# Where the eight attention up matmuls of a pair stand: two blocks of four, or one at each of eight places in the doubling levels

## The chip, the core and the metric

The kernel runs on one core of one Trainium2 chip. The metric is the device time of one execution in microseconds (us), and three runs of the kernel before the change took 1629.02, 1631.33 and 1635.49 us (median 1631.33). The engines are TensorE (PE in the profile; its weight loads are PEld), VectorE (DVE), ScalarE (ACT), GpSimd (POOL) and SyncE (SP), which here only issues DMAs. They work in parallel and wait for each other through semaphores; each of them takes its own instructions in program order.

## The reference, cut to what matters

One trunk layer over 384 tokens (128 context tokens and 256 latent ones, three tiles of 128): a norm and a combined input projection, two token mixers beside each other (a bidirectional RWKV-7 scan and grouped-query attention), a gated merge, and then top-4-of-32 experts. The part around the change is the mixer's end:

```
y_r, s_f, s_b = rwkv7_bidir(r, k, v, (wd_f, wd_b), (ad_f, ad_b), gd, (s0_f, s0_b), lp)
...
y_a = block_attention(rope_2d(qh), k_all, v_all)
merged = (jax.nn.sigmoid(gate_r) * (y_r @ lp["w_up_r"])
          + jax.nn.sigmoid(gate_a) * (y_a @ lp["w_up_a"]))
return merged @ lp["w_out"], kh, vh, s_f, s_b
```

The scan of one step is `S = S * w_t - (S kk_t) (kk_t a_t)^T + v_t k_t^T`, once forward and once backward over each sequence. The changed matmuls are `y_a @ w_up_a`: (384 x 512) by (512 x 1024), all fp32.

## The kernel before, in words

The program runs in stages: modulation, the input projection with the attention woven in (up to about 280 us), the RWKV scans (about 280 to 494 us), the merge and output projection (to about 563 us), second norm, router and placement (to about 620 us), and the expert blocks, which stream some 400 MB of weights.

The scans are written in chunk form, and run in three pairs (`pairs`). A pair p is one tile for the forward direction (d = 0) and one for the backward direction (d = 1). `bk(d, i)` is PSUM bank 4d + i, so each direction has four of the eight banks. A pair goes through these steps, on PE with the helpers `mm` and `quads`:

- the small low-rank matmuls (banks 4d and 4d + 1) for decay and in-context rate, then the cumulative sums (`cum`, `colm`), between them and after them elementwise work on DVE (L1728 to L1752) and exponentials on ACT (L1346 to L1351);
- 32 transposes (L722), copied out by ACT, and 64 Gram matmuls, which DVE masks into `AM` (L1760);
- one `quads` group for each direction into bank 4d + 3. A `quads` group is 16 fp32 matmuls of 64 x 64, which use quarters of the array;
- the doubling levels, l = 1 to 5 (`LEVELS` is 6), which invert a triangular matrix. In each level PE runs a group P for d = 0 and for d = 1 (bank 4d, operands `AM` and `XM`), and then a group D for d = 0 and for d = 1 (bank 4d + 2, operands `PM` and `XT`). DVE makes `PM[d]` from P's bank by a mask (L1777), makes the new `XT[d]` by subtracting D's bank (L1781), and turns it into `XM[d]` (L1784), which the next level's P waits for. Before the first level DVE makes the first `XT` (L1766, L1767) and the first `XM` (L1769);
- the state matmuls of two chunks, whose results DVE and ACT take up.

Into this sequence the attention's up matmuls were put, since they depend on none of it. For one tile they are eight: two column halves n of 512, each an accumulation of four (k = 0 to 3) over a stationary 128 x 128 block of `yaT` (in `first`) with a moving 128 x 512 of `w_up_a` (in `ring`). `up_a(j, n, bank)` did one half, by `up_half`, four matmuls in a row; ACT's `raised` copied the bank to `upa_out[j]` in `zbuf`. In pair 0 both halves stood between the last `quads` group and the first level. In pairs 1 and 2 half 0 stood behind the low-rank matmuls and half 1 before the first level. The order on each engine is that of the code; there is no planner. In the records of the trace one fp32 matmul is two MATMUL records (and two LDWEIGHTS), so a `quads` group is x32, and half an up projection x8.

What hangs on the end of the scans: everything behind them on PE, ACT, DVE and SP waits for `yrd` to reach 12, the last of the chunk results. The issue of the second half of `w_out`, `weights(("out", 1))` at L510, waits for `upad` to reach 6, all six up halves.

Of the kernel before, what the change touches and what calls it, by code (L numbers as in the profile page):

```python
# [29 lines left out]
P = 128  # L30
D = 1024
KC = D // P
NT = 3
# [21 lines left out]
CH = 512  # L55
# [18 lines left out]
LEVELS = 6  # L74
# [11 lines left out]
SLOT = KC * CH  # L86
# [71 lines left out]
def build(nc, a, o):  # L158
    ctx = ExitStack()
    with ctx:  # L160
# [216 lines left out]
        def landed(eng, key):  # L377
            i = turn[key]
            eng.wait_ge(s_wld[i % 3], 16 * (i // 3 + 1))
# [333 lines left out]
        def _(pe):  # L713
# [174 lines left out]
            def up_half(key, src, j, n, bank):  # L888
                w = at(ring, (turn[key, 0] + 1) % 3 * SLOT, 4, D)
                for k in range(4):  # L890
                    last = mm(bank, src[:, k, j * P:(j + 1) * P], w[:, k, n * CH:(n + 1) * CH], k == 0, k == 3)
                return last

            def up_a(j, n, bank):
                if j == n == 0:
                    landed(pe, ("upa", 0))
                    pe.wait_ge(S["yTc"], NT)
                up_half("upa", yaT, j, n, bank).then_inc(S["upad"], 1)

# [3 lines left out]
            for p, pair in enumerate(pairs):  # L903
# [8 lines left out]
                if p == 0:  # L912
                    turn_attended()
                else:
                    up_a(p, 0, bk(1, 2))
                for d, j in pair:
                    u = 2 * p + d
                    pe.wait_ge(S["lw"], u + 1)
                    if p == 0:
                        pe.wait_ge(S["yTc"], (1, NT)[d])  # L920
                    elif d == 1:
                        pe.wait_ge(S["yTc"], NT + 2 * p + 1)
                    mm(bk(d, 3), cum[:, 2 * d + 1, :], LW[d]).then_inc(S["lcum"], 1)
                    mm(bk(d, 2), cum[:, 2 * d, :], LW[d]).then_inc(S["lcum"], 1)
                    for c in range(4):
                        last = mm(bk(d, 0)[:, 4 * c:4 * c + 4], LW[d][:, c * P:(c + 1) * P], colm[:, 4 * d:4 * d + 4])
                    last.then_inc(S["lcum"], 1)
# [27 lines left out]
                if p == 0:  # L955
                    up_a(0, 0, bk(0, 1))
                    up_a(0, 1, bk(1, 1))
                else:
                    up_a(p, 1, bk(0, 1))
                for l in range(1, LEVELS):  # L960
                    for d, j in pair:
                        pe.wait_ge(s_x[d], NX * p + 2 * l)
                        if l > 1:
                            pe.wait_ge(s_pc[d], NP * p + l - 1)
                        quads(bank_block(bk(d, 0)), blocks(AM[d], 0), blocks(XM[d])).then_inc(s_p[d], 1)
                    for d, j in pair:
                        pe.wait_ge(s_pc[d], NP * p + l)
                        quads(bank_block(bk(d, 2)), blocks(PM[d]), blocks(XT[d])).then_inc(s_d[d], 1)
                pe.wait_ge(S["yTc"], NT + 2 * p + 2)
                for d, j in pair:  # L970
# [260 lines left out]
        def _(sc):  # L1231
# [101 lines left out]
            for p, pair in enumerate(pairs):  # L1333
# [4 lines left out]
                if p == 0:  # L1338
                    for j in range(NT):
                        turned(j, (B[2], B[7], B[6])[j], tile_of(yaT, j))  # L1340
                else:
                    raised(p, 0, bk(1, 2))
                for d, j in pair:
# [14 lines left out]
                for d, j in pair:  # L1358
                    sc.wait_ge(s_u[d], 3 * p + 1)
                    cp(flat(GM[d]), bk(d, 3)).then_inc(s_uc[d], 1)  # L1360
                if p == 0:
                    raised(0, 0, bk(0, 1))
                    raised(0, 1, bk(1, 1))
                else:
                    raised(p, 1, bk(0, 1))
                for d, j in pair:
# [766 lines left out]
```

## Time and profile before

| | us |
|---|---|
| median of three runs | 1631.33 |
| the profiled execution | 1628.82 |
| its span in the trace | 1626.9 |
| PE busy, share of the span | 1469.4, 90% |
| DVE busy | 524.0, 32% |
| ACT busy | 262.1, 16% |
| scans, from the first pair's levels to their end | about 305 to 494 |

A row of the timeline says when a run of like instructions began, how long it took, its engine, line, operation, tiles and count, and in brackets how long the engine had been idle before it and which instruction ended that idle time. A row of the chain gives start, duration and what the end of the program was waiting for in that stretch. Times in the rows are microseconds from the start of the span. L715 is the line inside `mm`, L719 that inside `mm_part`, L722 that inside `tr`; L1232 is ACT's copy helper.

### The profile page before, as it was taken

What the parts mean: (1) busy time and instruction counts of PE and PEld (TensorE: products, weight loads), DVE (VectorE), ACT (ScalarE), POOL (GpSimd) and SP (SyncE); (2) the same over time, 40 slices, a digit from 0 to 9 for tenths busy, and PEclk for the clock granted to TensorE, in tenths of its full rate; (3) what the DMA queues carried; (4) which work ended last, traced back from release to release, by engine and by line L of the source; (5) the groups of instructions that cost most, each with busy time, mean ns of one, the idle gap of its engine ahead of it and who ended that gap; (6) DMA issues with size and microseconds to landing.
All of it is one profiled execution on the core that took longest, in us unless ns stands there. A gap on an engine that the chain in (4) does not pass through costs nothing.

```text
span 1626.9 us, 26117 instructions
## 1 busy us (share of the span) xinstructions
PE 1469.4 (90%) x10008; PEld 706.3 (43%) x10009; DVE 524.0 (32%) x976; ACT 262.1 (16%) x514; POOL 98.9 (6%) x191
## 2 busy tenths in 40 slices
PE   4899998988987967999989999999998998998994
PEld 1777666777684442333323333333332332332331
DVE  3464544777877542101101101101011010110126
ACT  0332333221301200101101101111011010110110
POOL 1000000000001000000000000000000000000011
PEclk8799999999997967999999999999999999999996
DMA  9556835000016486999999999999999999999995
GB/s 364 200 189 239 324 133 187 2 9 3 2 55 220 171 329 272 421 421 421 421 421 421 421 422 420 422 421 421 421 420 423 420 421 420 419 421 419 419 411 190
DMA packets 97928, 510.78 MB, mean 314 GB/s; under 512 B 14752, under 2 KB 17072, under 8 KB 45160
## 3 DMA queue, kind: packets, MB, share of 16 engines
q1 hardware_dynamic: 82392, 479.03, 72.5%
q10 hardware_dynamic: 10624, 18.23, 3.0%
q0 software_dynamic: 4848, 12.59, 2.1%
q8 instruction: 50, 0.82, 0.2%
q14 instruction: 14, 0.11, 0.0%
HBM read 491.03 MB, written 22.71 MB: 316 GB/s over the span
## 4 chain that ended last, share of the span: by engine, by line
PE 60%; DMA 16%; SPq 10%; DVE 10%; issue 3%; ACT 1%; POOL 0%; DVEq 0%; ACTq 0%; POOLq 0%
PE bank L715 47%; PE bank L719 10%; SPq L594 9%; DMA ring<-w_moe_in 5%; DMA work<-w_moe_in 3%; DMA spare<-w_moe_in 3%; PE bank L722 3%; DMA zbuf<-w_ada 1%; DVE work L2051 1%; DMA work<-rows_d,dest 1%; DVE work L1781 1%; DMA work<-mods_d 1%; DVE work L1760 1%; DVE work L2052 1%; DVE work L1784 1%
## 5 line engine op out<-in xcount | busy, mean ns | idle before, releaser
L715 PE MATMUL bank<-work 64*64 64x64 f32 (+3 forms) x5134 | 528.9, 353 | 38.4 <-DMA work<-w_moe_in 11.2
L715 PEld LDWEIGHTS bank<-work 64*64 64x64 f32 (+2 forms) x5134 | 243.9, 136 | 286.5 <-issue 231.8
L715 PE MATMUL bank<-ring,work 128*64 128x512 f32 (+1 forms) x1376 | 352.8, 607 | 17.1 <-DMA ring<-w_moe_in 11.0
L2045 DVE TENSOR_SCALAR work<-bank 128x512 f32<-128x512 f32 x39 | 27.0, 692 | 753.1 <-PE bank L715 753.1
L715 PEld LDWEIGHTS bank<-ring,work 128*64 128x64 f32 (+1 forms) x1376 | 115.1, 145 | 224.9 <-issue 192.3
L1232 ACT ACTIVATE work<-bank 128x512 f32<-128x512 f32 (+2 forms) x223 | 110.8, 512 | 568.9 <-PE bank L715 323.3
L719 PE MATMUL bank<-parts 128*128 128x512 f32 (+1 forms) x720 | 168.1, 388 | 2.9 <-DVE parts L448 2.9
L715 PE MATMUL bank<-zbuf,work 64*64 64x64 f32 (+2 forms) x966 | 138.4, 388 | 12.5 <-DMA zbuf<-w_moe_in 4.5
L719 PEld LDWEIGHTS bank<-parts 128*128 128x128 f32 x720 | 129.3, 191 | 33.9 <-issue 5.2
L1462 ACT ACTIVATE work<-work 128x512 f32<-128x512 f32 x39 | 24.6, 630 | 469.8 <-DVE work L2045 469.8
L715 PEld LDWEIGHTS bank<-zbuf,work 64*64 64x64 f32 (+2 forms) x966 | 63.8, 139 | 77.0 <-issue 59.7
L722 PE MATMUL bank<-ident,work 128*128 128x128 f32 (+1 forms) x340 | 68.5, 319 | 22.1 <-DVE work L2052 11.2
L448 DVE TENSOR_TENSOR parts<-ring,parts 128x1024 fp32r<-128x1024 f32 (+1 forms) x40 | 45.7, 1145 | 76.7 <-ACT parts L443 76.7
L722 PEld LDWEIGHTS bank<-ident,work 128*128 128x128 f32 (+1 forms) x340 | 47.9, 179 | 49.6 <-DVE work L2052 32.5
L715 PE MATMUL bank<-spare,work 128*64 128x512 f32 (+1 forms) x256 | 61.3, 557 | 3.8 <-ACT work L1232 2.1
L680 POOL TENSOR_TENSOR half<-half 128x1 f32<-128x1 f32 x38 | 7.0, 183 | 847.0 <-PE bank L722 834.1
L715 PE MATMUL bank<-first,work 128*64 128x512 f32 x208 | 52.6, 607 | 2.0 <-DMA first<-w_moe_in 2.0
L443 ACT ACTIVATE parts<-ring 128x1024 fp32r<-128x1024 f32 (+1 forms) x40 | 39.6, 994 | 77.4 <-PE bank L719 73.6
L2051 DVE TENSOR_SCALAR work<-bank 128x256 f32<-128x256 f32 x78 | 32.9, 421 | 57.2 <-PE bank L715 57.2
L667 POOL DMA_INDIRECT zbuf<-h_d,slots x39 | 40.9, 1050 | 19.8 <-issue 19.8
L722 PEld LDWEIGHTS bank<-ident,zbuf 128*128 128x128 f32 x204 | 23.6, 150 | 41.8 <-issue 37.7
L715 PE MATMUL bank<-rowc 96*64 96x512 bf16 x234 | 39.9, 392 | 1.8 <-issue 1.8
(261 smaller groups left out, 859.8 us busy)
## 6 DMA issues: line engine op xcount, KB each, us to landing
work<-w_moe_in SPq DMA_DIRECT2D x108, 1024.0 KB, 22.8
ring<-w_moe_in SPq DMA_DIRECT2D x84, 1024.0 KB, 25.5
work<-w_moe_out SPq DMA_DIRECT2D x64, 1024.0 KB
ring<-w_moe_out SPq DMA_DIRECT2D x44, 1024.0 KB, 21.3
ring<-w_ada SPq DMA_DIRECT2D x11, 2048.0 KB, 7.7
zbuf<-w_moe_in SPq DMA_DIRECT2D x22, 1024.0 KB
first<-w_moe_in SPq DMA_DIRECT2D x21, 1024.0 KB
spare<-w_moe_in SPq DMA_DIRECT2D x21, 1024.0 KB
```

The source lines that it names most:

```text
L443: nc.scalar.activation(zpart(t, 0, n), z_quarter(t), ACT.Copy).then_inc(S["hi"], 1)
L448: eng.tensor_tensor(zpart(t, 1, n), z_quarter(t), zpart(t, 0, n), ALU.subtract)\
L594: sp.dma_start(place_of(turn_e, c), src).then_inc(s_place[(WC * turn_e + c) % NPLACE], 16)
L667: gp.indirect_dma_start(xg, None, h2_d.rearrange("t (h n) -> (t h) n", h=2), bass.IndirectOffsetOnAxis(ap=slots[:, 0:1], axis=0), bounds_c ...
L715: return pe.matmul(out, l, r, start=start, stop=stop)
L719: return pe.matmul(out, l, r, start=start, stop=stop, skip_group_check=True)
L722: return pe.transpose(out, src, ident[0:n, 0:n])
L1232: cp = lambda out, src, scale=1.0: sc.activation(out, src, ACT.Copy, scale=scale)
L1462: sc.activation(th, gl, ACT.Tanh, scale=ALPHA / 2).then_inc(S["thd"], 1)
L1760: tt(dst, bk(d, 2 * par + i).rearrange("p (c n) -> p c n", c=2), gramm[:, d:d + 1, :].broadcast_to([P, 2, 4 * HC]), M).then_inc(S["am"], 1)
L2045: ts(gl, B[0], LIMIT, None, ALU.min).then_inc(S["thd"], 1)
L2051: LL(ts(uu[:, seg], B[1][:, seg], LIMIT, -LIMIT, ALU.min, ALU.max))
```

## The change

The up matmuls of a pair are issued one by one: in each of the levels 1 to 4, one (half 0, k = l - 1, bank 1) between the P groups and the D groups, and one (half 1, bank 5) behind the D groups. `up_a` now takes k, and issues one matmul through `mm_part`, which is `mm` without the check that accumulation groups don't interleave; the instruction is the same. Level 5 has none. Half 0 of pairs 1 and 2 goes from behind the low-rank matmuls to the levels. ACT copies both halves behind the copies of `GM`, in every pair. The wait on `yTc` that protected bank 6 is gone with the half that used it. The number of matmuls and of copies is the same.

```
-            def up_a(j, n, bank):
-                if j == n == 0:
-                    landed(pe, ("upa", 0))
-                    pe.wait_ge(S["yTc"], NT)
-                up_half("upa", yaT, j, n, bank).then_inc(S["upad"], 1)
+            def up_a(j, n, k):
+                w = at(ring, (turn["upa", 0] + 1) % 3 * SLOT, 4, D)
+                ins = mm_part(bk(n, 1), yaT[:, k, j * P:(j + 1) * P], w[:, k, n * CH:(n + 1) * CH], k == 0, k == 3)
+                if k == 3:
+                    ins.then_inc(S["upad"], 1)
...
                 if p == 0:
                     turn_attended()
-                else:
-                    up_a(p, 0, bk(1, 2))
                 for d, j in pair:
                     u = 2 * p + d
                     pe.wait_ge(S["lw"], u + 1)
                     if p == 0:
                         pe.wait_ge(S["yTc"], (1, NT)[d])
-                    elif d == 1:
-                        pe.wait_ge(S["yTc"], NT + 2 * p + 1)
...
                 if p == 0:
-                    up_a(0, 0, bk(0, 1))
-                    up_a(0, 1, bk(1, 1))
-                else:
-                    up_a(p, 1, bk(0, 1))
+                    landed(pe, ("upa", 0))
                 for l in range(1, LEVELS):
                     for d, j in pair:
                         pe.wait_ge(s_x[d], NX * p + 2 * l)
                         if l > 1:
                             pe.wait_ge(s_pc[d], NP * p + l - 1)
                         quads(bank_block(bk(d, 0)), blocks(AM[d], 0), blocks(XM[d])).then_inc(s_p[d], 1)
+                    if l < LEVELS - 1:
+                        up_a(p, 0, l - 1)
                     for d, j in pair:
                         pe.wait_ge(s_pc[d], NP * p + l)
                         quads(bank_block(bk(d, 2)), blocks(PM[d]), blocks(XT[d])).then_inc(s_d[d], 1)
+                    if l < LEVELS - 1:
+                        up_a(p, 1, l - 1)
...
@@ (ScalarE)
-                else:
-                    raised(p, 0, bk(1, 2))
...
-                if p == 0:
-                    raised(0, 0, bk(0, 1))
-                    raised(0, 1, bk(1, 1))
-                else:
-                    raised(p, 1, bk(0, 1))
+                for n in range(2):
+                    raised(p, n, bk(n, 1))
```

On PE, at the start of pair 1's levels, this stood before. Banks 0 and 4 take the P groups of the two directions, banks 2 and 6 the D groups, `ring,first` marks the up matmuls, and a row x16 is one `quads` group:

```order
L715 MATMUL bank3<-zbuf,work 64x64 x16
L715 MATMUL bank7<-zbuf,work 64x64 x16
L715 MATMUL bank1<-ring,first 128x512 x4
L715 MATMUL bank0<-work 64x64 x16
L715 MATMUL bank4<-work 64x64 x16
L715 MATMUL bank2<-work 64x64 x16
L715 MATMUL bank6<-work 64x64 x16
L715 MATMUL bank0<-work 64x64 x16
L715 MATMUL bank4<-work 64x64 x16
```

At the same place of PE's program now:

```order
L715 MATMUL bank7<-zbuf,work 64x64 x16
L715 MATMUL bank0<-work 64x64 x16
L715 MATMUL bank4<-work 64x64 x16
L719 MATMUL bank1<-ring,first 128x512
L715 MATMUL bank2<-work 64x64 x16
L715 MATMUL bank6<-work 64x64 x16
L719 MATMUL bank5<-ring,first 128x512
L715 MATMUL bank0<-work 64x64 x16
L715 MATMUL bank4<-work 64x64 x16
L719 MATMUL bank1<-ring,first 128x512
```

The block of four ahead of the first P group is gone, and one up matmul stands between each two P groups and the D groups behind them, another behind the D groups.

At the start of pair 1, behind the low-rank matmuls (`spare` into banks 0, 4, 1, 5), PE had half 0 in bank 6 ahead of the cumulative sums:

```order
L715 MATMUL bank1<-spare 128x512
L715 MATMUL bank5<-spare 128x512
L715 MATMUL bank6<-ring,first 128x512 x4
L715 MATMUL bank3<-work,spare 128x512
L715 MATMUL bank2<-work,spare 128x512
L715 MATMUL bank0<-colm,work 128x4 x4
```

And now:

```order
L722 MATMUL bank4<-ident,work 64x128 x4
L715 MATMUL bank0<-spare 128x512
L715 MATMUL bank4<-spare 128x512
L715 MATMUL bank1<-spare 128x512
L715 MATMUL bank5<-spare 128x512
L715 MATMUL bank3<-work,spare 128x512
```

The cumulative sums follow the low-rank matmuls directly.

## Rows read from the trace of the kernel before

**Rows 1.** The page, part 4: the chain that ended last, by engine.
```profile
PE 60%; DMA 16%; SPq 10%; DVE 10%; issue 3%; ACT 1%; POOL 0%; DVEq 0%; ACTq 0%; POOLq 0%
```

**Rows 2.** The chain in order of time, one level of pair 1: start, duration, what.
```profile
384.01 2.11 PE bank L715 x64
...
386.14 0.70 DVE work L1781
...
386.90 0.60 issue
387.50 0.66 DVE work L1781
...
388.18 0.72 DVE work L1784
...
388.95 2.11 PE bank L715 x64
```

**Rows 3.** Timeline of PE, pair 1, up half 1 and the first levels.
```profile
373.36 1.15 PE L715 MATMUL bank<-zbuf,work 64*64 64x64 f32 x32 [1.24 <-DVE work L1760]
374.43 3.70 PE L715 MATMUL bank<-ring,first 128*128 128x512 f32 x8
378.06 4.02 PE L715 MATMUL bank<-work 64*64 64x64 f32 x128
...
384.01 3.09 PE L715 MATMUL bank<-work 64*64 64x64 f32 x96 [0.17 <-DVE work L1784]
387.63 1.15 PE L715 MATMUL bank<-work 64*64 64x64 f32 x32 [0.53 <-DVE work L1784]
```

**Rows 4.** Timeline of DVE, pair 1: first XM, first and last XT of d = 0.
```profile
374.66 0.71 DVE L1769 STREAM_TRANSPOSE work<-work 128x512 f32<-128x512 f32 x1
...
376.71 0.71 DVE L1769 STREAM_TRANSPOSE work<-work 128x512 f32<-128x512 f32 x1
...
381.20 0.69 DVE L1781 TENSOR_TENSOR work<-work,bank 128x512 f32<-128x512 f32 x1 [0.32 <-PE bank L715]
...
400.95 0.69 DVE L1781 TENSOR_TENSOR work<-work,bank 128x512 f32<-128x512 f32 x1 [0.24 <-PE bank L715]
```

**Rows 5.** Timeline of PE, pair 0, both up halves.
```profile
298.49 7.13 PE L715 MATMUL bank<-ring,first 128*128 128x512 f32 x16
305.56 0.62 PE L715 MATMUL bank<-work 64*64 64x64 f32 x14
```

**Rows 6.** Timeline of DVE, pair 0: the second first XM, the first XT subtraction.
```profile
300.76 0.71 DVE L1769 STREAM_TRANSPOSE work<-work 128x512 f32<-128x512 f32 x1
...
308.69 0.69 DVE L1781 TENSOR_TENSOR work<-work,bank 128x512 f32<-128x512 f32 x1 [0.32 <-PE bank L715]
```

**Rows 7.** Timeline of DVE, pair 2, the same two.
```profile
446.07 0.71 DVE L1769 STREAM_TRANSPOSE work<-work 128x512 f32<-128x512 f32 x1
...
450.57 0.69 DVE L1781 TENSOR_TENSOR work<-work,bank 128x512 f32<-128x512 f32 x1 [0.32 <-PE bank L715]
```

**Rows 8.** Timeline of PE, pair 2, inside its second level.
```profile
456.39 1.84 PE L715 MATMUL bank<-work 64*64 64x64 f32 x55 [0.56 <-issue]
```

**Rows 9.** Timeline of PE, pair 1: the 32 transposes ahead of the Gram matmuls.
```profile
363.44 3.82 PE L722 MATMUL bank<-ident,work 128*128 128x128 f32 x32
```

**Rows 10.** Timeline of DVE, pair 1: the last product that is transposed.
```profile
365.86 0.68 DVE L1745 TENSOR_TENSOR work<-zbuf,work 128x512 f32<-128x512 f32 x1
```

**Rows 11.** Windows: busy us of PE, PEld, DVE, ACT, POOL (records), granted clock, DMA.
```profile
347.90:354.40 6.50, 5.23 (x16) 2.43 (x16) 1.61 (x3) 1.62 (x3) 0.00 (x0) 0.50 0.20 43
416.00:422.00 6.00, 5.22 (x126) 5.09 (x124) 3.37 (x8) 0.98 (x4) 0.00 (x0) 1.00 0.02 4
487.90:508.10 20.20, 13.91 (x63) 8.63 (x62) 15.18 (x28) 0.60 (x1) 2.46 (x2) 0.58 0.50 158
```

**Rows 12.** The chain, behind the output projection.
```profile
564.74 16.23 DMA work<-mods_d
```

**Rows 13.** The page, part 6: loads of 2 MB into a ring slot, us to landing.
```profile
ring<-w_ada SPq DMA_DIRECT2D x11, 2048.0 KB, 7.7
```

## The prediction

> **What bounds the kernel now.** I read the page's chain first: PE carries 60% of it, DVE 10%, DMA and its issue 26% [rows 1]. Most of that is the expert stage, which the change does not touch. It matters only that every stage behind the scans starts from their end (`yrd`), so that a microsecond gained or lost in the scans should reach the end of the program.
>
> Then the chain inside one doubling level of pair 1, between one start of P(d=1) and the next [rows 2]. Two `quads` groups on PE, P(d=1) and D(d=0), take 384.01 to 386.14; DVE then subtracts for d=0 (386.14), turns it, subtracts for d=1 (387.50) and turns that (388.18), and P(d=1) of the next level starts at 388.95. A level is 4.94 us, and in it PE and DVE take turns. The reader is to see that DVE's subtraction for d=0 is released by D(d=0), and that D(d=0) stands directly behind P(d=1) on PE: the three groups P(d=1), D(d=0), D(d=1) run without a break (3.09 us, x96), while PE's idle time lies behind the D groups, 0.53 us, and between the two P groups, 0.17 us [rows 3]. So of the two new places in a level, the one behind the D groups has 0.7 us of idle time to fill, and the one between P and D has none: it stands on the chain.
>
> **What one up matmul costs.** Eight in a row took 298.49 to 305.56, 7.07 us [rows 5]; four in a row took 374.43 to 378.06, 3.63 us [rows 3]. The difference gives 0.86 us for one inside a block, and leaves 0.19 us that each block pays once. One more piece: a lone group lasts 1.15 us from its first start to its last result, while groups in a row follow each other by (3.09 - 1.15)/2 = 0.97 us; but the up block started 1.07 us behind the group ahead of it (373.36 to 374.43) [rows 3], so the entry costs 0.10 us more. A single up matmul among `quads` groups is then S = 0.86 + 0.19 + 0.10 = 1.15 us of PE. The trace has no lone one. The bounds: 0.86 us, if nothing is paid at the change; and 0.86 + 0.29 + 2 x 0.18 = 1.51 us, if on both sides the 0.18 us by which a group's last result trails its spacing (1.15 - 0.97) is waited out on top. I take 1.15, since both blocks, of four and of eight, stood between `quads` groups too and agree on it.
>
> The Trainium skill, TensorEngine Tiling (Array Packing), section Tiling Modes, says that a change of the tiling mode, not of the tile alone, drains the engine. This speaks against the change, which makes 24 excursions out of the levels' 64 x 64 mode where there were three; the rows show 0.29 us for one excursion, which fits that rule. Without a drain the price would be the low bound.
>
> **A level with its two up matmuls.** I count from the start of P(d=1). By DVE: group 0.97, up 1.15, D(d=0) until its last result 1.15, release 0.01, which puts the subtraction for d=0 at 3.28; from there DVE needs what it needs now, 386.14 to 388.95 = 2.81 [rows 2]: 6.09 us. By PE: four groups and two up matmuls, 4 x 0.97 + 2 x 1.15 = 6.18 us. PE is the later one, barely. A level goes from 4.94 to 6.18 us, and PE then has no idle time in it.
>
> **The pairs, from the first level to the subtraction (d=0) of the fifth.** Without a block ahead, the first P(d=1) waits only for the second L1769: it may start 0.71 + 0.06 us behind that one's start. Then 3.28 us to the first subtraction, three times 6.18 to the fourth level's, and 6.18 - 1.15 = 5.03 to the fifth's, which has no up matmul ahead of its D: 26.85 us in all. Before, four levels of 4.94 us followed the first subtraction: 19.76 us, or 381.20 to 400.95 in pair 1 [rows 4].
> - Pair 0: 300.76 + 0.77 + 26.85 = 328.38, against 308.69 + 19.76 = 328.45 [rows 6]. The removed block of eight pays for the eight singles: -0.07 us.
> - Pair 1: 376.71 + 0.77 + 26.85 = 404.33, against 400.95 [rows 4]: +3.38 us. Only a block of four stood here.
> - Pair 2: 446.07 + 0.77 + 26.85 = 473.69, against 450.57 + 19.76 + 0.50 [rows 7]: +2.86 us. The 0.50 is the one irregular stop in the second level, idle 0.56 us with no releaser, which delayed it [rows 8]; I take it as not coming again.
> The sum is +6.17 us. The start is sound if the first P(d=0) is early enough: its XM is there at 375.37 [rows 4], so it is.
>
> **What comes out of the start of pairs 1 and 2.** Half 0, again 3.6 us of PE, stood there beside DVE's elementwise run, which goes on without a gap (no bracket in [rows 10]) up to the products that PE transposes. The cumulative sums get earlier, the products do not. The last product of pair 1 ends at 366.54; four transposes of 3.82/32 us behind it would end at about 367.08, where they now end at 367.26 [rows 9, 10]. So removing it gives back the 0.1 to 0.2 us by which PE lagged, in each of the two pairs: -0.25 us. That is why the sum is bad: these four matmuls per pair were nearly free where they stood, and now go onto the chain.
>
> **What is hidden.** ACT's two copies of 0.6 us wait for the fourth level's up matmuls, and have the whole fifth level of about 5 us before PE writes banks 1 and 5 again. The issue of the second w_out half moves from before pair 2's levels to the end of their fourth, near 475; it is read only in the output projection, behind the scans' end near 500, and SP has nothing queued behind it but waits for that end. A load of this size lands in 7.7 us [rows 13]. The longest single wait behind the scans, 16.23 us for a DMA [rows 12], is issued by work that shifts along with everything else, with the weight stream that it competes with. I cost these at nothing; if the w_out load had no cover, its 7.7 us would come on top, and nothing points there.
>
> **Sum.** 6.17 - 0.25 = +5.9 us. The profiled execution, 1628.82 us with a span of 1626.9, would become 1634.7; it lay 2.5 us under the median of the three runs, so against 1631.33 the forecast is 1637.2 us.
>
> **The rivals.**
> A. *The switch is dearer in single use (slower by over 0.5%).* Each pair's length depends on S eight times, so the sum moves by 24 x (S - 1.15). At S = 1.51 it is 5.9 + 8.6 = +14.5 us: 1645.8 us. It crosses 0.5% (8.2 us) already at S = 1.25. For it: no lone one is in the trace. Against it: the 0.29 us is the same for blocks of four and eight.
> B. *The switch is free.* At S = 0.86 DVE sets the level: 0.97 + 0.86 + 1.15 + 0.01 + 2.81 = 5.80 us. From its start a pair takes 2.99 + 3 x 5.80 + 4.94 = 25.33 us, 1.52 less than above; 6.17 - 4.56 - 0.25 = +1.4 us: 1632.7 us. For it: weights might load behind the groups. Against: the start at 1.07 us in place of 0.97, and the 0.19 us.
> C. *The clock pays it back (not slower).* The granted clock falls to its lower level of 1.2 GHz at the end of pair 0 and again at 487.9, after PE had stood 3 us in pair 2's tail; in pair 1's tail it stayed at 2.4 GHz [rows 11]. If the fuller levels shift the falls away, 5.23 us of PE work in the first stretch take half, saving 2.6, and the 13.91 us at a mean of 0.58 in the second save 13.91 x 0.42 = 5.8: 8.4 us at most. Some of it, the gate matmuls among it, lies beside DVE's work; I take three quarters, 6.3: 5.9 - 6.3 = -0.4, or 1630.9 us. It decides from the point where both falls vanish. Against it: the tails keep their idle times, and the fall could just as well come to pair 1's tail, at a cost of 1 to 3 us.
> D. *The change doesn't do what it says*, say the single matmuls slip into PE's 0.7 us idle time and delay no D group. In-order PE excludes this for the first of the two; the order rows show it ahead of bank 2.
>
> **Chances.** The forecast's mechanism at S near 1.15 (+4 to +8 us): 0.60. A: 0.20. B or something between: 0.10. C: 0.08, D or a gain that I don't see: 0.02. 0.5% of the time, about what a measurement of this kernel can tell from no change, is 8.2 us, so the likeliest case lies inside it, though slower. Faster by over 0.5%: 0.02. Slower by over 0.5%: A, and the upper edge of the forecast with the runs' own spread, 0.26. Within: 0.72. The likeliest case's own range is 1635 to 1639.5. The range takes in B and C below and half of A above: 1631 to 1642.5.
>
> **What would show it.** In the profile after, P(d=1) to P(d=1) inside levels 2 to 4 should be near 6.2 us (5.8 in B, 6.9 in A), with no idle time of PE behind the D groups; DVE should show a gap of about 1.1 to 1.4 us more per level ahead of L1781 or L1777. The first subtraction of pair 0 should come at 304.8 in place of 308.69, 3.9 us sooner, that of pair 1 by 0.4 us. The stretch from the low-rank matmuls to the Gram matmuls should be 0.1 to 0.2 us shorter. The scans should end near 500 in place of 494, and all behind it be shifted by the same amount. I am wrong if levels stay under 5.5 us, or if the stage behind the scans changes its own length by more than 2 us.

## The result: 13 to 14 us slower, 0.6 to 0.8%

The changed kernel took 1644.28 us in the median of four runs (1640.44 to 1646.49), the kernel before 1630.17 (1628.19 to 1635.49): a ratio of 1.0076, 95% interval 1.0057 to 1.0095. A second batch gave 1642.78 against 1629.76 us, 1.0064 (1.0044 to 1.0084). The forecast was 1637.2 us with a range up to 1642.5, so the direction was right, and the change cost more than twice what was forecast.

The profiled execution of the changed kernel is the slowest of its first four runs, 1646.49 us with a span of 1644.6, which is 17.7 us over the span of before. It shows every part of the loss, together more of it than in the median run.

**The levels.** The chain of the changed kernel inside pair 0's levels (start, duration, what):

```profile
309.21 1.05 PE bank L719 x2
310.27 2.01 PE bank L715 x64
312.28 1.06 PE bank L719 x2
313.34 2.02 PE bank L715 x64
315.35 1.06 PE bank L719 x2
```

A level is 315.35 - 309.21 = 6.14 us in place of 4.94 [rows 2], all of it PE: two pairs of groups and two up matmuls. DVE, which took its turn in every level before, has left the chain. One up matmul takes 1.06 us, and the two groups ahead of it 2.01 us, 0.07 more than two groups at the spacing of 0.97 us that [rows 3] gives.

**The first level of pair 1.** Timeline of PE, the place of [rows 3]:

```profile
376.06 1.15 PE L715 MATMUL bank<-zbuf,work 64*64 64x64 f32 x32 [1.24 <-DVE work L1752]
378.13 4.02 PE L715 MATMUL bank<-work 64*64 64x64 f32 x64 [0.92 <-DVE work L1761]
382.09 2.07 PE L719 MATMUL bank<-ring,first 128*128 128x512 f32 x2
384.09 2.30 PE L715 MATMUL bank<-work 64*64 64x64 f32 x64
386.32 1.13 PE L719 MATMUL bank<-ring,first 128*128 128x512 f32 x2
```

Two P groups now take 4.02 us, and a single up matmul 2.07 us, where the next one takes 1.13. PE idled 1.24 us ahead of the last group before them, as it did in the kernel before [rows 3], and then 0.92 us more, where the block of four stood and began without a wait. Windows of the changed kernel (columns as in [rows 11]; the granted clock is third from the end) show why, and where else:

```profile
343.60:357.40 13.80, 11.47 (x79) 8.30 (x76) 5.10 (x11) 1.80 (x4) 0.00 (x0) 0.51 0.09 19
377.60:384.60 7.00, 6.39 (x76) 4.58 (x78) 3.84 (x6) 0.26 (x1) 0.00 (x0) 0.51 0.01 2
425.60:436.00 10.40, 9.53 (x66) 6.74 (x64) 3.44 (x7) 0.98 (x2) 0.00 (x0) 0.51 0.01 2
456.60:460.00 3.40, 3.33 (x64) 3.14 (x64) 2.51 (x4) 0.00 (x0) 0.00 (x0) 0.54 0.00 0
504.40:528.00 23.60, 17.98 (x80) 11.13 (x81) 15.85 (x29) 0.60 (x1) 3.27 (x2) 0.57 0.49 151
```

TensorE's clock was at 1.2 GHz in five stretches in place of two [rows 11]: the tail of each pair, and the starts of the levels of pairs 1 and 2. The fall in pair 0's tail comes about 4 us sooner than before and lasts twice as long.

**A stop behind the levels of pair 2.** Timelines of SP and of PE, changed kernel:

```profile
482.77 0.39 SPq L510 DMA_DIRECT2D ring<-w_out  x1
```

```profile
491.20 0.97 PE L715 MATMUL bank<-work 64*64 64x64 f32 x29 [2.28 <-issue]
```

PE stands still for 2.28 us from 488.92, released by no semaphore. In [rows 8] such a stop was 0.56 us. It falls into the end of the 2 MB load of w_out, whose issue the change moved and which takes 9.0 us from its issue to its landing here.

**Where the 17.7 us are.** The start of the first Gram mask of each pair and of the first reduction behind the scans on DVE, first before, then now:

```profile
292.48 4.88 DVE L1760 TENSOR_TENSOR work<-bank,gram 128x512 f32<-128x512 f32 x8 [1.61 <-PE bank L715]
...
368.42 4.88 DVE L1760 TENSOR_TENSOR work<-bank,gram 128x512 f32<-128x512 f32 x8 [0.94 <-PE bank L715]
...
437.79 4.88 DVE L1760 TENSOR_TENSOR work<-bank,gram 128x512 f32<-128x512 f32 x8 [0.94 <-PE bank L715]
...
494.19 0.69 DVE L1843 TENSOR_REDUCE stat<-ky 128x8 f32<-128x512 f32 x1
```

```profile
292.88 4.88 DVE L1752 TENSOR_TENSOR work<-bank,gram 128x512 f32<-128x512 f32 x8 [1.61 <-PE bank L715]
...
371.13 4.88 DVE L1752 TENSOR_TENSOR work<-bank,gram 128x512 f32<-128x512 f32 x8 [0.93 <-PE bank L715]
...
449.50 4.88 DVE L1752 TENSOR_TENSOR work<-bank,gram 128x512 f32<-128x512 f32 x8 [0.94 <-PE bank L715]
...
512.51 0.69 DVE L1835 TENSOR_REDUCE stat<-ky 128x8 f32<-128x512 f32 x1
```

| stretch | before | now | difference |
|---|---|---|---|
| up to the first mask | 292.48 | 292.88 | +0.40 |
| mask of pair 0 to that of pair 1 | 75.94 | 78.25 | +2.31 |
| mask of pair 1 to that of pair 2 | 69.37 | 78.37 | +9.00 |
| mask of pair 2 to the end of the scans | 56.40 | 63.01 | +6.61 |
| from there to the end of the span | 1132.7 | 1132.1 | -0.6 |

The stage behind the scans passes the delay on without change, as the prediction assumed. The rest of the question is how the 17.9 us in the scans split between the levels, the clock and the stop; they hold more falls of the clock than a second profile of the same kernel does.

### The profile page after: what moved, and what is told of

It reads as the page before. It is cut to its first block, busy times and chain, and to the rows that moved or that the text cites. A ratio compares the mean times of both kernels' runs of the same rounds, so it can differ in the third digit from the quotient of the medians.

```text
span 1644.6 us, 26115 instructions
## 1 busy us (share of the span) xinstructions
PE 1484.0 (90%) x10008; PEld 713.0 (43%) x10009; DVE 524.6 (32%) x976; ACT 263.3 (16%) x514; POOL 98.9 (6%) x191
## 4 chain that ended last, share of the span: by engine, by line
PE 63%; DMA 16%; DVE 10%; SPq 8%; issue 3%; ACT 1%; POOL 0%; DVEq 0%; ACTq 0%; POOLq 0%
PE bank L715 48%; PE bank L719 11%; SPq L594 8%; DMA ring<-w_moe_in 5%; DMA work<-w_moe_in 3%; DMA spare<-w_moe_in 3%; PE bank L722 3%; DMA zbuf<-w_ada 1%; DVE work L2043 1%; DMA work<-rows_d,dest 1%; DMA work<-mods_d 1%; DVE work L1752 1%; DVE work L2044 1%; DVE ring L2056 0%; DMA rows_d<-work 0%
## 5 line engine op out<-in xcount | busy, mean ns | idle before, releaser
L715 PE MATMUL bank<-work 64*64 64x64 f32 (+3 forms) x5134 | 541.6, 358 | 33.9 <-DMA work<-w_moe_in 8.1
L715 PEld LDWEIGHTS bank<-work 64*64 64x64 f32 (+2 forms) x5134 | 251.2, 140 | 300.0 <-issue 243.4
L715 PE MATMUL bank<-zbuf,work 64*64 64x64 f32 (+2 forms) x966 | 143.0, 392 | 12.7 <-DMA zbuf<-w_moe_in 4.7
L715 PEld LDWEIGHTS bank<-zbuf,work 64*64 64x64 f32 (+2 forms) x966 | 67.8, 145 | 77.2 <-issue 59.6
```

The source lines that it names most:

```text
L715: return pe.matmul(out, l, r, start=start, stop=stop)
```

## Experiments

All ratios are to the kernel before, on the same chip, with 95% intervals. In the diffs `up_a(p, n, k, bank)` is the changed kernel's single up matmul, with an optional bank.

### The changed kernel again

> The changed kernel once more, as the reference of this batch. All theories: about 14 us over before (ratio 1.0076). If the excess beyond the 5.9 us of the prediction comes from TensorE's clock, the falls to the lower level in its profile may stand at other places than in the first profile, while the levels stay at 6.14 us each where the clock is at 2.4 GHz.

Measured: 1642.78 us, 1.0064 (1.0044 to 1.0084). The levels are 6.13 to 6.14 us again. The low stretches stand elsewhere (windows of this execution; those of pair 2's tail, from 500 us on, are left out):

```profile
302.00:306.00 4.00, 3.77 (x36) 2.26 (x37) 1.44 (x3) 0.00 (x0) 0.00 (x0) 0.57 0.00 0
350.00:357.00 7.00, 5.67 (x16) 2.43 (x16) 1.76 (x4) 2.18 (x4) 0.00 (x0) 0.51 0.18 39
377.00:381.00 4.00, 3.46 (x62) 3.27 (x64) 3.08 (x5) 0.19 (x1) 0.00 (x0) 0.57 0.02 4
432.00:435.50 3.50, 3.50 (x7) 1.52 (x7) 3.37 (x7) 0.84 (x3) 0.00 (x0) 0.51 0.00 0
452.50:456.00 3.50, 3.34 (x34) 2.28 (x34) 1.37 (x3) 0.00 (x0) 0.00 (x0) 0.51 0.00 0
486.50:490.50 4.00, 4.00 (x96) 4.00 (x95) 0.75 (x2) 0.60 (x1) 0.00 (x0) 0.57 0.02 4
```

Here the clock fell at the start of all three pairs' levels, while the tails of pairs 0 and 1 lost less. The same program thus gets its falls at other places from run to run, near places where PE has idled. PE's stop behind the levels is there again, 2.32 us. The Trainium skill, TensorE: Matmul & The Clock Gate, section What's actually happening, says that the activity monitor runs freely and does not start with the kernel, so that the place of a change of clock varies. The two profiles agree that it varies; here whole falls come and go, such as the 10.4 us in pair 1's tail, of which 3.5 us are left.

### Only the places behind the D groups

```
-                    if l < LEVELS - 1:
-                        up_a(p, 0, l - 1)
...
+                else:                                  # behind the low-rank matmuls, pairs 1 and 2
+                    for k in range(4):
+                        up_a(p, 0, k, bk(1, 2))
...
+                    for k in range(4):                 # ahead of the levels, pair 0
+                        up_a(0, 0, k)
```

> Half 1 singly behind the D groups of levels 1 to 4, as in the changed kernel; half 0 back in its old place (pairs 1 and 2) and a block of four before the levels in pair 0. Nothing stands between the P and the D groups. Theory 'chain' alone: a level takes 4.94 us again (PE 4 x 0.97 + 1.06 = 4.94, tie), the first P(d=1) comes 3.4 us sooner in pair 0 and 1.55 us in pairs 1 and 2: 6.5 us under before, ratio 0.996. Theory 'clock' (the block that is gone leaves PE idle ahead of the levels, and the clock falls there and earlier in the pairs' tails): falls at the starts of the levels of pairs 1 and 2, 3 us each, total from -3 to +3 us against before. Theory 'instruction loading behind the w_out load' (the load now starts at the end of pair 2's fourth level): a stop of PE of about 2 us behind the levels of pair 2, 1.8 us more than before.

Measured: 1630.05 us, 1.0000 (0.9988 to 1.0012): the whole loss is gone, but the time is not the 6.5 us under before that the chain alone gives. Timeline of PE, pair 1:

```profile
372.27 5.60 PE L715 MATMUL bank<-work 64*64 64x64 f32 x128 [0.92 <-DVE work L1769]
377.81 1.12 PE L719 MATMUL bank<-ring,first 128*128 128x512 f32 x2
378.86 4.02 PE L715 MATMUL bank<-work 64*64 64x64 f32 x128
382.81 1.12 PE L719 MATMUL bank<-ring,first 128*128 128x512 f32 x2
```

From one up matmul to the next it is 5.0 us, against 4.94 for a level of before: behind the D groups an up matmul costs 0.07 us. But the four groups of the first level take 5.60 us where four take 4.02 two rows on: the clock was low again behind PE's idle time (granted 0.55 from 371.6 to 375.4), and the stop behind the levels of pair 2 was 2.27 us. The profile shows where the gain went: from DVE's mask to the fifth subtraction the three pairs took 5.7 us less than before, while from pair 2's fifth subtraction to the end of the scans it took 27.94 us in place of 23.36, 4.6 us more. There PE stopped, and the clock was low for some 3.5 us directly behind the stop. Both theories have their share, that of the w_out load the larger.

### Only the places between P and D

```
+                for k in range(4):
+                    up_a(p, 1, k)
                 for l in range(1, LEVELS):
...
-                    if l < LEVELS - 1:
-                        up_a(p, 1, l - 1)
```

> Half 0 singly between the P and the D groups, half 1 as a block of four before the levels in each pair. Theory 'chain': 4.94 + 1.06 = 6.0 us a level, pair 0 +0.8, pairs 1 and 2 +4.1 each, together +9 us against before (ratio 1.0055). Theory 'clock': the block before the levels covers the idle time, so no fall at the levels' starts; only tails may differ. Theory 'instruction loading': +1.8 us more, a stop of about 2 us behind pair 2's levels, in all +11 us.

Measured: 1643.56 us, 1.0077 (1.0055 to 1.0100): as slow as the changed kernel, with half of its interleaving. Timeline of PE, pair 1:

```profile
384.39 1.15 PE L715 MATMUL bank<-work 64*64 64x64 f32 x32 [0.60 <-DVE work L1776]
385.71 1.15 PE L715 MATMUL bank<-work 64*64 64x64 f32 x32 [0.17 <-DVE work L1776]
386.79 1.13 PE L719 MATMUL bank<-ring,first 128*128 128x512 f32 x2
387.85 2.08 PE L715 MATMUL bank<-work 64*64 64x64 f32 x64
390.53 1.15 PE L715 MATMUL bank<-work 64*64 64x64 f32 x32 [0.60 <-DVE work L1776]
```

A level is 390.53 - 384.39 = 6.14 us and PE idles 0.77 us in it: the up matmul delays D, D delays DVE's subtraction, and PE waits for DVE as before. With the place between taken, the places behind the D groups come for nothing, which is why the changed kernel's level is no longer than this one. The clock stayed at 2.4 GHz at the starts of the levels, where the block covers the idle time, as the theory has it; in the tails it was low from 348.5, 423.5 and 502 us. So the fall in pair 1's tail, which made that tail 41.22 us in place of 36.84, comes with the block in place too; it goes far to explain why the time lies above the 9 us that the chain gives. The stop behind the levels was only 0.15 us here, against the 2 us expected.

### Both single matmuls behind the D groups

```
-                    if l < LEVELS - 1:
-                        up_a(p, 0, l - 1)
...
                     if l < LEVELS - 1:
+                        up_a(p, 0, l - 1)
                         up_a(p, 1, l - 1)
```

> Both single up matmuls of a level stand behind its D groups, none between P and D. The amount of PE work is the changed kernel's with one excursion less a level. Theory 'chain': a level is now PE's 4 x 0.97 + 2 x 0.86 + 0.29 = 5.9 us, or, where DVE needs the 0.7 us idle time only, 4.94 + 1.1 to 1.3; 0.2 us a level less than 6.14, in all 2 to 3 us under the changed kernel. Rival, that the place between P and D is itself the loss and not PE's total: near the time of before.

Measured: 1638.45 us, 1.0043 (1.0029 to 1.0058). Its chain in pair 1:

```profile
382.81 3.95 PE bank L715 x128
386.76 1.91 PE bank L719 x4
388.67 3.95 PE bank L715 x128
```

A level is 5.86 us, all PE. So the place is not the loss in itself: a level of 4.94 us has 0.7 us of idle PE, one up matmul nearly fits, two don't. The second matmul of an excursion costs 0.86 us, the first 1.06, which bears out the 0.86 + 0.19 of the prediction.

### Filler where the block stood

```
+                else:
+                    for k in range(4):
+                        mm_part(bk(0, 1), first[:, 0:P], first[:, k * P:k * P + CH], True, True)
```

> The changed kernel, with four filler matmuls of 128x512 (their result is overwritten) where the block of pairs 1 and 2 stood. Theory 'chain' alone: the first P(d=1) of both pairs comes 1.6 us later, so 3.2 us slower than the changed kernel. Theory 'clock': the falls at the starts of the levels of pairs 1 and 2 vanish from the profile, which gives back about 3 us each: 0 to 3 us faster than the changed kernel in spite of 7 us more matmul work.

Measured: 1644.05 us, 1.0076 (1.0056 to 1.0096), no different from the changed kernel. The profile shows what happened. Windows over the starts of the levels of pairs 1 and 2:

```profile
376.00:386.00 10.00, 10.00 (x171) 6.85 (x172) 6.29 (x10) 0.60 (x1) 0.00 (x0) 1.00 0.01 2
452.00:462.00 10.00, 8.70 (x142) 5.70 (x138) 7.78 (x13) 1.19 (x2) 0.00 (x0) 1.00 0.01 2
```

The falls there are gone, and 7 us of useless matmul work cost nothing that the runs can tell. This is one profile, and falls vary between runs, but it fits that the uncovered idle time sets them off. The first subtractions of pairs 1 and 2 came 13.91 and 13.89 us behind their masks; in the changed kernel's profile it was 14.38 and 12.88, and 12.38 where the clock was up: what the clock gave back, the later start of P took. The falls in the tails of pairs 0 and 1 did not go with the others. They stand where they stood in the changed kernel, from 343.5 and 425.5 us, so the missing block is not shown to be their cause.

### The block left out of the kernel before

```
-                    up_a(p, 1, bk(0, 1))
+                    mm(bk(0, 1)[:, 0:4], yaT[:, 0, p * P:(p + 1) * P], yaT[:, 0, 0:4]).then_inc(S["upad"], 1)
```

> The kernel before, with half 1 of pairs 1 and 2 left out but for one 128x4 matmul (its result is not the up projection), nothing in the levels. Theory 'chain' alone: the first P(d=1) comes 1.3 to 1.55 us sooner in each of the two pairs, about 3 us faster than before. Theory 'clock': with the block gone PE idles ahead of the levels and the clock falls there or in the tails, which costs 1 to 3 us a pair: same as before or slower, with the falls in the profile at about 377 and 446 us.

Measured: 1634.88 us, 1.0013 (1.0002 to 1.0025): 7 us of matmul work less, and not faster but slightly slower. This kernel does not compute half of the up projection of two tiles. The chain alone was to give 3 us; the first subtraction of pairs 1 and 2 came 0.9 and 1.6 us sooner after the mask. Windows:

```profile
377.00:381.00 4.00, 3.83 (x76) 3.64 (x78) 2.62 (x5) 0.20 (x1) 0.00 (x0) 0.57 0.02 4
418.00:428.50 10.50, 9.73 (x81) 7.39 (x74) 3.68 (x7) 0.43 (x1) 0.00 (x0) 0.51 0.01 2
```

One fall at the start of pair 1's levels, as expected, and one in pair 1's tail, where before the clock had stayed up. The first fall cost 0.7 us (the first subtraction 11.86 us behind the mask, in pair 2 with the clock up 11.18), the second 3.9 us (pair 1's tail 40.72 in place of 36.84). Nothing stood in the levels of this kernel, so this is the clock without the interleaving. Four of the twelve runs took 1628.7 to 1631.4 us and eight 1633.1 to 1636.8, the profiled one among the eight.

### A filler in the tails

```
+                    if k == 1:
+                        mm_part(bk(0, 0), first[:, 0:P], first[:, 0:CH], True, True)
```

> The changed kernel, with one filler matmul of 128x512 in each pair's second chunk, where PE waits 1.21 us for DVE. Theory 'clock, set off by idle time': the falls in the tails of pairs 0 and 1 (13.6 and 10.2 us at the lower level in the first profile) vanish or get shorter, up to 5 us faster than the changed kernel. Rival, that the falls come from something other than that wait: falls as before, same time or 0.3 us slower.

Measured: 1641.72 us, 1.0068 (1.0046 to 1.0091), with a spread from 1636.3 to 1647.9. The median tells nothing apart. The profiled execution, 1636.61 us, was a lucky one and is the cleanest view of the chain there is: PE's clock stayed at 2.4 GHz from the first level of pair 1 through the whole of its tail and pair 2's levels. Masks of its pairs, and the fifth subtraction of pair 2:

```profile
293.48 4.88 DVE L1754 TENSOR_TENSOR work<-bank,gram 128x512 f32<-128x512 f32 x8 [1.61 <-PE bank L715]
...
368.50 4.88 DVE L1754 TENSOR_TENSOR work<-bank,gram 128x512 f32<-128x512 f32 x8 [1.04 <-PE bank L715]
...
440.64 4.88 DVE L1754 TENSOR_TENSOR work<-bank,gram 128x512 f32<-128x512 f32 x8 [0.94 <-PE bank L715]
...
476.44 0.69 DVE L1775 TENSOR_TENSOR work<-work,bank 128x512 f32<-128x512 f32 x1 [0.32 <-PE bank L715]
```

Pair 0 takes 75.02 us (before 75.94), pair 1 72.14 (69.37), pair 2 35.80 from its mask to the fifth subtraction (33.04, which is 470.83 - 437.79): -0.92, +2.77 and +2.76, together +4.6 us. This sum still holds the tails of pairs 0 and 1, with the filler in them and, in pair 0, a low stretch of 10.5 us; up to the fifth subtractions alone the three pairs cost 5.9 us, which is the price of the matmuls' places with the clock up. The changed kernel differs from this one by the filler alone, and its profile took 3.2 us more in pair 0 and 6.2 us more in pair 1.

### The w_out load: late, in pieces, and moved in the kernel before

Issued behind the scans and behind the gate loads, in the changed kernel:

```
-            weights(("out", 1))
             sp.wait_ge(S["yrd"], NSTEP)
...
             sp.dma_start(gld[1], gates_d[1]).then_inc(S["gld"], 16)
+            weights(("out", 1))
```

> The changed kernel, with the load of the second half of w_out issued behind the scans (after the gate loads) in place of at the end of pair 2's fourth level. Theory 'instruction loading behind that load': PE's stop of 2.3 us without a releaser behind the levels of pair 2 vanishes, and the kernel is about 2 us faster than the changed one, unless the load comes late for the output projection. Rival, that the stop has to do with the program's place alone (code that is always fetched late there): the stop of 2.3 us stays, same time.

Measured: 1639.36 us, 1.0044 (1.0030 to 1.0058). There is no stop in PE at that place.

In four pieces of 0.5 MB, one for each level of pair 2:

```
+                    for q in range(4):
+                        sp.wait_ge(S["upad"], (5, 6, 7, 9)[q])
+                        sp.dma_start(ring_slot[i % 3][:, 2 * q:2 * q + 2, :], src[:, 2 * q:2 * q + 2, :]).then_inc(s_wld[i % 3], 16)
```

> The changed kernel, with the w_out load cut into four loads of 0.5 MB, each issued when its part of the slot is free, one per level of pair 2. Theory 'instruction loading': the stop of 2.3 us vanishes or falls under 0.5 us, about 2 us faster than the changed kernel (ratio 1.005 to 1.006), without the late arrival that a load behind the scans could bring. Chain and clock: unchanged, so it stays slower than before.

Measured: 1638.29 us, 1.0047 (1.0029 to 1.0065), and no stop either.

The kernel before, with only the issue held back to the D groups of pair 2's fourth level:

```
                     sp.wait_ge(S["upad"], 2 * NT)
+                    sp.wait_ge(s_d[1], 3 * NP - 1)
```

> The kernel before, with only the issue of the second half of w_out held back until the D groups of pair 2's fourth level, where the changed kernel has it. Theory 'instruction loading behind that load': PE's stop of 0.56 us in pair 2's second level goes, and one of about 2.3 us appears some 6 us behind the issue: 1.7 us slower than before (ratio 1.001). Rival 'the stop belongs to the place of the matmuls': no such stop, same time.

Measured: 1634.18 us, 1.0014 (1.0002 to 1.0026). The stop appears in a kernel whose matmuls are those of before:

```profile
471.38 5.18 PE L716 MATMUL bank<-work 64*64 64x64 f32 x197 [0.17 <-DVE work L1785]
479.04 3.25 PE L716 MATMUL bank<-work 64*64 64x64 f32 x81 [2.48 <-issue]
```

Three runs agree: take the load away from the end of pair 2's levels and the stop goes, put it there and it comes. It began at 476.56, 6.9 us behind the issue (469.64), near the 6 us expected, when most of the 2 MB had landed.

That PE waits there for its own instructions, held up by the load, can be read from the DMA records. The profile's DMA table has a queue of the kind `instruction`, q8, whose packets are 16 KB each. The packets next to the stop:

| kernel | packet before, start | next packet, start to end | PE stopped |
|---|---|---|---|
| changed | 481.01 | 488.79 to 489.75 | 488.92 to 491.20 |
| before, w_out moved | 468.69 | 476.47 to 477.52 | 476.56 to 479.04 |
| before | 444.07 | 453.77 to 454.79 | 455.83 to 456.39 |
| only the places between | 481.77 | 485.51 to 486.57 | 487.84 to 487.99 |

In all seven profiles with a stop of over 2 us the packet starts 7.2 to 8.0 us behind the one before it, with the load in between, and PE goes on 1.3 to 1.5 us behind its end. With the load issued behind the scans, these packets follow each other in this stretch in 3.5 to 4.8 us, and PE doesn't stop. In the kernel with only the places between, the packet came 3.7 us behind the last one, and the stop was 0.15 us. I call the load's part shown, and the late instruction packet as its way well supported; what stays open is that no record names the engine that a packet is for.

The stop also has a follower. Directly behind it the clock was low for 3.5 to 4 us in four of the seven profiles (the changed kernel again, only the places behind the D groups, the filler in the tails, and this kernel). From pair 2's fifth subtraction to the end of the scans these four took 27.0 to 28.0 us, the other three 24.8 to 26.7, and the kernel before 23.36. So the load's new place can cost up to 4.6 us, and not the 2.3 of the stop alone.

### Putting the matmuls where PE idles

```
+                    if d == 0:                          # between the two quads groups ahead of the levels
+                        up_a(p, min(p, 1), 0, bk(0, 1))
+                for k in range(1, 4 if p == 0 else 3):  # ahead of the first P group
+                    up_a(p, min(p, 1), k, bk(0, 1))
...
+                    if p == 0 and l < LEVELS - 1:       # behind the D groups
+                        up_a(0, 1, l - 1)
+                    elif p and l == 1:
+                        up_a(p, 1, 3, bk(0, 1))
```

Half 0 of pairs 1 and 2 is in its old place.

> The up matmuls where PE idles beside the chain: one between the two quads groups ahead of the levels (1.24 us idle), two (three in pair 0) ahead of the first P group, the rest singly behind D groups (level 1 in pairs 1 and 2, levels 1 to 4 in pair 0); half 0 of pairs 1 and 2 in its old place. Chain: pair 0 about 4.1 us sooner, pairs 1 and 2 1.5 us each, less 0.07 us for each single behind D: 6.8 us under before. Clock: the idle time ahead of the levels is covered, so no falls there, only in the tails, whose place may differ by some us. Instruction loading: the w_out load starts in pair 2's second level, near its place of before: a stop of about 0.5 us. Ratio 0.996.

Measured: 1624.28 us, 0.9961 (0.9943 to 0.9978): faster than both kernels, 6.4 us under before, where the chain promised 6.8.

With the filler of the tails added:

> The same with one filler matmul of 128x512 in each pair's second chunk (1.21 us idle). If idle time sets off the falls of the clock in the tails: fewer low stretches before 480 us, up to 3 us faster than without the filler; otherwise the same.

Measured: 1620.71 us, 0.9941 (0.9918 to 0.9964), the fastest of all, though its interval overlaps that of the version without filler. Timeline of PE in pair 1:

```profile
368.77 1.15 PE L715 MATMUL bank<-zbuf,work 64*64 64x64 f32 x32
369.85 1.13 PE L719 MATMUL bank<-ring,first 128*128 128x512 f32 x2
371.17 1.15 PE L715 MATMUL bank<-zbuf,work 64*64 64x64 f32 x32 [0.19 <-DVE work L1766]
372.24 1.98 PE L719 MATMUL bank<-ring,first 128*128 128x512 f32 x4
374.16 4.21 PE L715 MATMUL bank<-work 64*64 64x64 f32 x128
378.30 1.13 PE L719 MATMUL bank<-ring,first 128*128 128x512 f32 x2
```

The 1.24 us gap between the two groups is down to 0.19, and the first level starts with the clock up.

## Why the prediction was right in sign and wrong in size

**The chain and the price of one matmul: right.** A level was forecast at 6.18 us and is 6.14; the single matmul was to cost 1.15 us of PE and costs 1.06 with 0.07 at its entry. From the mask to the fifth subtraction the three pairs took 35.80, 35.81 and 35.80 us with the clock up (filler in the tails) against 35.96, 32.53 and 33.04 before: -0.16, +3.28 and +2.76, forecast -0.07, +3.38 and +2.86. This is 5.9 us measured against 6.17 forecast. The -0.25 us from the starts of pairs 1 and 2 can't be told apart in the tails, which vary by more. So the term of the places held, and the miss lies in the two terms that the sum put at nothing.

**Rival B (free switch) fell, and so did A (dearer switch):** 0.19 + 0.07 us for each excursion, single or not. The measured time lies near A's 1645.8 us, but by another way: S is 1.13, not 1.51.

The two profiles of the changed kernel can be split at DVE's instructions in the same way, in us, with two of the experiments beside them. A tail here is the stretch from the fifth subtraction to the next pair's mask, in pair 2 to the end of the scans:

| stretch | before | changed | changed, again | filler where the block stood | filler in the tails |
|---|---|---|---|---|---|
| pair 0, mask to fifth subtraction | 35.96 | 35.80 | 37.38 | 35.79 | 35.80 |
| pair 0, tail | 39.98 | 42.45 | 39.91 | 42.44 | 39.22 |
| pair 1, mask to fifth subtraction | 32.53 | 37.80 | 36.39 | 37.33 | 35.81 |
| pair 1, tail | 36.84 | 40.57 | 36.76 | 41.26 | 36.33 |
| pair 2, mask to fifth subtraction | 33.04 | 36.31 | 37.30 | 37.32 | 35.80 |
| pair 2, tail | 23.36 | 26.70 | 27.99 | 24.75 | 27.91 |
| together | 201.71 | 219.63 | 215.73 | 218.89 | 210.87 |

The 14.0 us of the second profile, which is near the median loss, are then 5.9 for the places, 3.7 for falls of the clock at the starts of the levels, 4.6 in pair 2's tail, and -0.2 in the tails of pairs 0 and 1. The 17.9 us of the first profile are 5.9, 2.5, 3.3 and 6.2.

**"What is hidden": wrong for the w_out load, the first step that failed.** I had asked only whether the load lands in time, and costed it at nothing. It does land in time. What I did not ask is what else uses the DMA engines while it runs. [rows 8] showed the warning, a stop of 0.56 us without a releaser some 8 us behind the issue of that very load; I put it down as irregular and subtracted it. At its new place the stop is 2.3 us, and with the low clock that can follow it pair 2's tail is 3.3 and 4.6 us longer. Taking the load away gave about 3 to 5 us in two versions (1.0044 and 1.0047, against 1.0064 and 1.0076 of the changed kernel in other batches), though these intervals overlap in part.

**The clock at nothing in the sum: the second step that failed.** I let the clock vary only in the tails, as rival C and mainly as a gain, called a loss of 1 to 3 us possible in one sentence, and gave it neither a chance of its own nor a place in the range. "The start is sound" checked only that XM is there in time. I moved the first P group up to its XM, and did not say that the block of four had filled PE's wait for that XM, 0.92 us in pair 1, and followed the 1.24 us of idle time ahead of it with dense work. Without it the clock fell at the start of some pair's levels in six of the seven profiles of kernels with single matmuls in the levels and no block ahead of pairs 1 and 2, and at none in the six profiles where matmuls stood there; the kernel before fell there too when its block was left out. This cost 2.5 and 3.7 us in the two profiles of the changed kernel.

**The falls in the tails of pairs 0 and 1: open.** They cost 6.2 us in the first profile and nothing in the second, of the same program. The one in pair 0's tail is no work of the change: the kernel before with only w_out moved, whose program is that of before up to pair 2, took 42.52 us there. The one in pair 1's tail stayed when a filler stood in the block's place and came with the block itself in the kernel with only the places between (41.22 us); no run shows what sets it off. Rival C had named it, at 1 to 3 us; it was 3.7. These falls are also a reason why the runs of one kernel differ by some us.

**The stage behind the scans: right**, within 0.6 us.

## What to carry to other kernels

Before moving work out of a block, ask what the block covers: in a chain where two engines take turns, a place is cheap only if the idle time at that very place is as long as the work, and idle time that opens elsewhere can cost the clock what the chain gains. Fill TensorE's idle places with the movable matmuls first, and only then the places inside the loop. When a semaphore count that gates a large load moves, look at what runs on the other engines while the load is in flight, down to stops with no releaser.

## What the hardware showed beyond this

- TensorE's clock fell behind idle times of 0.9 to 1.2 us at the starts of the levels, with 3 to 7 us of work at half speed each time, and up to 13.8 us in a tail; a matmul 128x512 in fp32 then took 2.07 us in place of 1.13. The same 1.24 us of idle time with a block of four behind it left the clock up [rows 3].
- Whole falls come and go between executions of one program: pair 0's tail took 39.98 and 42.52 us in two kernels that are the same up to there.
- Removing 7 us of matmul work made a kernel 0.13% slower, and adding 7 us of filler to another cost nothing.
- A 2 MB load beside a long run of distinct PE instructions went with a stop of PE of 2.1 to 2.7 us in seven of the eight profiles in which it was issued late in pair 2; moved away or cut into four it went with none. In those seven a 16 KB packet of the instruction queue came 7.2 to 8.0 us behind the one before, and PE went on 1.3 to 1.5 us behind its end.
